# Nine of sixteen down stages computed with seven block products in place of eight

## The chip, the cores and the metric

One NeuronCore of a Trainium2 chip runs the kernel. The metric is device time in microseconds (us) of one execution; the time of a kernel is the median of its runs.

## The reference

The kernel computes one inference step of a decoder layer, for a prompt of 2048 tokens and 32 sample tokens, all in fp32 and 1024 wide. A mixing sub-layer comes first (one input projection, four mixers, one output projection). What matters here is the second half, a dense MLP with an inner width of 4096:

```python
f = rms_norm(x, g_ffn_pre)
f = jnp.square(jax.nn.relu(f @ w_up)) @ w_down      # (2048+32, 1024) @ (1024, 4096), then @ (4096, 1024)
x = x + rms_norm(f, g_ffn_post)
```

## The kernel before, in words

**Tiles and stages.** The prompt is cut into four blocks of 512 tokens (`b` = 0 to 3; the last block takes the 32 sample tokens with it). The inner width of 4096 is cut into four quarters of 1024 (`q` = 0 to 3). For each `b` and `q` there is a U stage, which makes u = relu(f @ w_up)² for 1024 inner columns, and a D stage, which multiplies u by the matching 1024 rows of w_down and adds the result to `f2_sb`. In the D stage of `q` = 3 the output projection of the next block is put in between. A U and a D stage together are called a round here.

**Panels.** Weights come in panels of 1024 rows by 256 columns (1 MB), four to a stage, in the order of the list `order`. A panel goes through the same steps in every stage: SyncE loads it to one of two buffers of `raw`; ScalarE (ACT) rounds it to `w_hi` (L702); VectorE (DVE) makes the rest, `w_lo` = `raw` - `w_hi` (L1161); TensorE (PE) takes both. `raw`, `w_hi` and `w_lo` each have two buffers, so the rounding of panel j+2 waits for the last matmul of panel j, and the load of panel j+2 for the subtraction of panel j.

**Products.** fp32 accuracy comes from three matmuls for each pair of tiles: high by high, low by high, high by low (`three`, L1873 to L1875). In the U stage the weights are stationary and 512 tokens move: a panel has 2 tiles of 128 inner columns, each 8 steps x 3 matmuls of 512 columns into one PSUM bank. ACT takes each bank through ReLU (L976) and square (L978) to one of two buffers `square`, DVE splits that into `u_hi` (a cast, L1564) and `u_lo` (L1568). In the D stage u is stationary and the 256 columns of w_down move: a panel is 4 token tiles x 8 steps x 3 = 96 matmuls, two token tiles to a bank, and a stage is 384 matmuls. DVE adds each bank to `f2_sb` (`d_add`, L1590); at `q` = 0 ACT copies instead (`d_copy`, L993).

**Order around the change.** Each engine runs a program written out by hand in its own order. In DVE's, `u_panel` and `token_panel` put the split of panel j+2 ahead of the last piece of panel j. Six PSUM banks (`mm`) are used in turn for U and D. GpSimd (POOL) computes nothing after the first microseconds; its queue only issues transfers: of the mixers' outputs (`mixc`, `mix_in`), of x and x2 to `x_in` (`rows_in`), of x2 and y to HBM (`results`). At the end of the first U stage come small steps for the 32 sample tokens, whose last result `conv_s` is stored from POOL's queue (L690); the first D stage waits for that store where `f2_sb` lies over the buffers of the first phase.

The functions that the diff touches, and their callers:

## Time and profile before

| | |
|---|---|
| median of 3 runs | 2186.59 us (2186.30 to 2190.09) |
| the profiled execution | 2184.32 us |
| its span, first to last instruction | 2182.4 us, granted clock 0.989 |
| PE busy / DVE busy / ACT busy / POOL busy | 96% / 50% / 35% / 5% |
| one U stage (`b` < 3), one D stage (`b` < 3, `q` < 3) | 44.15 us, 43.98 us |

A PE that is 96% busy leaves 87 us of the span in which no matmul runs. The lengths of the stages come from the timeline of PE, from the first matmul of a stage to the first of the next. Busy time counts overlapping matmuls once; the mean duration of one matmul is longer than the distance between two, since they are pipelined. DVE's and ACT's instructions don't overlap by more than 0.1 us, so their durations can be added.

### The profile page before, as it was taken

What the parts mean: (1) busy time and instruction counts of PE and PEld (TensorE: products, weight loads), DVE (VectorE), ACT (ScalarE), POOL (GpSimd) and SP (SyncE); (2) the same over time, 40 slices, a digit from 0 to 9 for tenths busy, and PEclk for the clock granted to TensorE, in tenths of its full rate; (3) what the DMA queues carried; (4) which work ended last, traced back from release to release, by engine and by line L of the source; (5) the groups of instructions that cost most, each with busy time, mean ns of one, the idle gap of its engine ahead of it and who ended that gap; (6) DMA issues with size and microseconds to landing.
All of it is one profiled execution on the core that took longest, in us unless ns stands there. A gap on an engine that the chain in (4) does not pass through costs nothing.

```text
span 2182.4 us, 32665 instructions
## 1 busy us (share of the span) xinstructions
PE 2095.6 (96%) x14201; PEld 1908.3 (87%) x14201; DVE 1099.4 (50%) x1505; ACT 754.7 (35%) x1160; POOL 107.7 (5%) x190
## 2 busy tenths in 40 slices
PE   6999999996999999999999999999999999999998
PEld 5877777786799898989898899899898989999998
DVE  3687777877623333564333346523334564334344
ACT  4424232234433323443323244332323443323142
POOL 2011111110000000000000000000000000000000
PEclk9999999997999999999999999999999999999999
DMA  7854656563232333344332344533333333222221
GB/s 254 284 212 161 223 178 213 174 204 126 70 118 96 97 97 126 131 149 155 97 97 97 97 136 155 170 101 97 97 97 118 108 108 136 94 81 84 92 78 61
DMA packets 184835, 287.40 MB, mean 132 GB/s; under 512 B 5967, under 2 KB 162292, under 8 KB 176484
## 3 DMA queue, kind: packets, MB, share of 16 engines
q1 hardware_dynamic: 160868, 169.99, 24.3%
q0 software_dynamic: 22784, 114.28, 14.9%
q8 instruction: 112, 1.84, 0.3%
q10 hardware_dynamic: 1040, 1.05, 0.1%
q14 instruction: 31, 0.25, 0.0%
HBM read 245.01 MB, written 40.57 MB: 131 GB/s over the span
## 4 chain that ended last, share of the span: by engine, by line
PE 65%; DVE 4%; ACT 3%; DMA 2%; issue 1%; POOL 0%; ACTq 0%; POOLq 0%; DVEq 0%
PE mm L1875 21%; PE mm L1873 21%; PE mm L1874 21%; DVE w_lo L1161 1%; ACT w_hi L702 1%; DMA mixc<-mixT_scratch 1%; PE mm L1882 1%; PE mm L1881 1%; DMA x_in<-in_x_prompt 0%; ACT junk_y L1003 0%; DVE conv_s L1779 0%; DVE f_sb L1590 0%; PE tr L2111 0%; ACT square L976 0%; DVE o_sb L1524 0%
## 5 line engine op out<-in xcount | busy, mean ns | idle before, releaser
L1161 DVE TENSOR_TENSOR w_lo<-raw,w_hi 128x2048 fp32r<-128x2048 f32 x152 | 348.5, 2293 | 644.6 <-ACT w_hi L702 644.6
L1873 PE MATMUL mm<-act_hi,w_hi 128*128 128x512 f32 (+2 forms) x1728 | 631.3, 365 | 8.1 <-DVE act_lo L1204 5.3
L1875 PE MATMUL mm<-act_hi,w_lo 128*128 128x512 f32 (+2 forms) x1728 | 631.0, 365 | 0.0
L1874 PE MATMUL mm<-act_lo,w_hi 128*128 128x512 f32 (+2 forms) x1728 | 624.7, 362 | 0.0
L1873 PE MATMUL mm<-w_hi,u_hi 128*128 128x256 f32 x2048 | 567.9, 277 | 1.7 <-DVE u_lo L1568 0.9
L1874 PE MATMUL mm<-w_lo,u_hi 128*128 128x256 f32 x2048 | 565.5, 276 | 0.0
L1875 PE MATMUL mm<-w_hi,u_lo 128*128 128x256 f32 x2048 | 565.4, 276 | 0.0
L702 ACT ACTIVATE w_hi<-raw 128x2048 fp32r<-128x2048 f32 x152 | 290.8, 1913 | 559.9 <-PE mm L1875 464.1
L1873 PEld LDWEIGHTS mm<-w_hi,u_hi 128*128 128x128 f32 x2048 | 384.4, 188 | 4.2 <-DVE u_lo L1568 3.8
L1874 PEld LDWEIGHTS mm<-w_lo,u_hi 128*128 128x128 f32 x2048 | 384.5, 188 | 0.5
L1875 PEld LDWEIGHTS mm<-w_hi,u_lo 128*128 128x128 f32 x2048 | 384.4, 188 | 0.0
L1873 PEld LDWEIGHTS mm<-act_hi,w_hi 128*128 128x128 f32 x1728 | 326.9, 189 | 60.2 <-issue 12.2
L1874 PEld LDWEIGHTS mm<-act_lo,w_hi 128*128 128x128 f32 x1728 | 327.0, 189 | 57.0 <-issue 2.4
L1875 PEld LDWEIGHTS mm<-act_hi,w_lo 128*128 128x128 f32 x1728 | 326.3, 189 | 50.7
L1873 PE MATMUL mm<-w_hi,act_hi 128*128 128x256 f32 x640 | 179.8, 281 | 7.5 <-DVE w_lo L1161 4.4
L1874 PE MATMUL mm<-w_lo,act_hi 128*128 128x256 f32 x640 | 178.0, 278 | 0.0
L1875 PE MATMUL mm<-w_hi,act_lo 128*128 128x256 f32 x640 | 178.0, 278 | 0.0
L976 ACT ACTIVATE square<-mm 128x512 f32<-128x512 f32 (+2 forms) x160 | 81.9, 512 | 244.5 <-PE mm L1875 237.6
L1215 DVE SCALAR_TENSOR_TENSOR conv<-g_ext,cst,conv 128x512 f32<-128x512 f32 x240 | 163.1, 746 | 0.7 <-ACT conv L826 0.7
L1564 DVE CAST u_hi<-square 128x512 fp32r<-128x512 f32 (+1 forms) x160 | 59.2, 370 | 145.1 <-ACT square L978 145.0
L1873 PEld LDWEIGHTS mm<-w_hi,act_hi 128*128 128x128 f32 x640 | 121.4, 190 | 8.9 <-DVE w_lo L1161 5.0
L1874 PEld LDWEIGHTS mm<-w_lo,act_hi 128*128 128x128 f32 x640 | 121.4, 190 | 0.6 <-issue 0.5
(269 smaller groups left out, 1512.8 us busy)
## 6 DMA issues: line engine op xcount, KB each, us to landing
raw<-in_w_ffn_up SPq DMA_DIRECT2D x64, 1024.0 KB, 5.3
raw<-in_w_ffn_down SPq DMA_DIRECT2D x64, 1024.0 KB, 5.2
w_hi<-whi_scratch POOLq DMA_DIRECT2D x24, 1024.0 KB, 5.2
w_lo<-wlo_scratch POOLq DMA_DIRECT2D x24, 1024.0 KB, 7.8
raw<-in_w_out SPq DMA_DIRECT2D x16, 1024.0 KB, 5.2
whi_scratch<-w_hi POOLq DMA_DIRECT2D x8, 1024.0 KB, 8.6
wlo_scratch<-w_lo POOLq DMA_DIRECT2D x8, 1024.0 KB, 10.7
mixc<-mixT_scratch POOLq DMA_DIRECT2D x16, 512.0 KB, 6.2
```

The costliest lines, as they stand in the source:

```text
L702: SC.activation(w_hi[:, s, :, :], raw[:, s, :, :], ACT.Copy).then_inc(hi_ready, 1)
L976: SC.activation(square[:, at % 2, 0:c1 - c0], mm[bank][:, 0:c1 - c0], ACT.Relu).then_inc(bank_free[bank], 1)
L1161: DVE.tensor_tensor(w_lo[:, s, :, :], raw[:, s, :, :], w_hi[:, s, :, :].bitcast(fp32), ALU.subtract)\
L1215: DVE.scalar_tensor_tensor(out=c, in0=g_ext[:, t, k:k + N1], scalar=col("conv_w", 2 * k + t), in1=c, op0=ALU.mult, op1=ALU.add).then_inc(c ...
L1564: DVE.tensor_copy(u_hi[:, k, c0:e], square[:, at % 2, 0:e - c0]).then_inc(u_hi_ready, 1)
L1873: PE.matmul(out, whi, xhi, start=(k == 0), stop=False)
L1874: PE.matmul(out, whi, xlo, start=False, stop=False)
L1875: return PE.matmul(out, wlo, xhi, start=False, stop=(k == K - 1))
L1881: PE.matmul(bank[0:2 * NS, 0:PC], x[:, k, :], whi, start=(k == 0), stop=False)
L1882: last = PE.matmul(bank[0:NS, 0:PC], x[:, k, 0:NS], wlo, start=False, stop=False)
```

## The change

In the D stages of `b` < 3 and `q` < 3 the product u @ w_down of 512 x 1024 by 1024 x 1024 is done by blocks. u is cut into 2 x 2 blocks A of 256 tokens by 512 inner rows (even tiles of 128 inner columns against odd ones), the weights into 2 x 2 blocks B of 512 inner rows by 512 columns. Winograd's form of Strassen's scheme then needs seven products of blocks, of these pairs:

| | left | right |
|---|---|---|
| part 0 | A11 | B11 |
| part 1 | S1 = A21 + A22 | T1 = B12 - B11 |
| part 2 | S2 = S1 - A11 | T2 = B22 - T1 |
| part 3 | A12 | B21 |
| part 4 | S3 = A11 - A21 | T3 = B22 - B12 |
| part 5 | S4 = A12 - S2 | B22 |
| part 6 | A22 | B21 - T2 (its sign is taken care of in the sums) |

Such a stage is called a W stage here. It has two halves (p = 0, 1) of 256 of each block's 512 columns, and seven products a half, each of 24 matmuls of 256 columns into one bank: 2 x 7 x 24 = 336 matmuls in place of 384. Who does what:

- SyncE loads eight pieces of 512 KB a stage in place of four of 1 MB.
- GpSimd makes the four sums of weight blocks of a half in place in `raw` (L764, L767, L769, L777), eight instructions of 128 x 1024 a stage.
- ACT and DVE split each part of the weights (128 x 1024) into high and low: 14 parts a stage, of which parts 0 and 1 of the first half lie at the end of the U stage's third panel.
- DVE makes the sums of u and splits all of them (`sums_1` to `sums_4`), in place of one cast and one subtraction a tile.
- DVE takes the products to seven sums `w_sum`, which lie in `f2_sb` and in `mixc`; at `q` = 0 it copies, ACT no longer does. `w_result` adds them up in the U stage of `q` = 3 (seven additions of 128 x 1024). The loads of `mixc` for the next block wait for that.
- The y tiles of the block before are done two each after panels 0 and 1 of the U stage, in place of one after each panel. The rest of the diff joins four semaphores to others and is left out below, as is the renumbering of buffers.

```diff
+        w_dn_7 = w_down[0].rearrange("(q k e p) c -> q e p k c", p=P, k=K // 2, e=2)
+        def wait_part(eng, j, i):
+            if i >= 4:
+                wait_bank(eng, j, i - 4)
+            elif order[j][3] == 1:
+                wait_bank(eng, j - 1, i + 3)
+            else:
+                wait_panel(eng, j - 2 + i // 2)
...
         @block.sync
+                        else:
+                            sp.wait_ge(lo_ready, split_no[j - 1] + 4)
+                            sp.dma_start(quarter(raw, b11), block_source(j, 0, 0)).then_inc(raw_full[b11], 16)
+                            sp.wait_ge(w_sums, 4 * w_no[j])
+                            sp.dma_start(quarter(raw, b12), block_source(j, 0, 1)).then_inc(raw_full[b12], 16)
+                            sp.wait_ge(lo_ready, split_no[j - 1] + 5)
+                            sp.dma_start(quarter(raw, b22), block_source(j, 1, 1)).then_inc(raw_full[b22], 16)
+                            sp.wait_ge(lo_ready, split_no[j - 1] + 6)
+                            sp.dma_start(quarter(raw, b21), block_source(j, 1, 0)).then_inc(raw_full[b21], 16)
...
+                    elif order[j - 1][0] == "W":
+                        sp.wait_ge(w_sums, 4 * (w_no[j - 1] + 1))
+                        sp.wait_ge(lo_ready, split_no[j - 1] + 5)
...
         @block.gpsimd
+            def weight_sums(j):
+                pool.wait_ge(raw_full[raw_at[j][2]], 16 * no12)
+                pool.wait_ge(lo_ready, split_no[j])
+                GP.tensor_tensor(b11, b12, b11, ALU.subtract).then_inc(w_sums, 1)
+                pool.wait_ge(raw_full[raw_at[j][3]], 16 * no22)
+                pool.wait_ge(w_sums, n + 1)
+                GP.tensor_tensor(b12, b22, b12, ALU.subtract).then_inc(w_sums, 1)
+                pool.wait_ge(lo_ready, split_no[j] + 1)
+                GP.tensor_tensor(b11, b22, b11, ALU.subtract).then_inc(w_sums, 1)
+            def weight_sum_4(j):
+                pool.wait_ge(w_sums, n + 3)
+                pool.wait_ge(lo_ready, split_no[j] + 3)
+                GP.tensor_tensor(b21, b21, b11, ALU.subtract).then_inc(w_sums, 1)
...
         @block.scalar
+            def part_hi(j, i):
+                wait_part(act, j, i)
...
+                if i in (1, 2, 4, 6):
+                    act.wait_ge(w_sums, 4 * w_no[j] + {1: 1, 2: 3, 4: 2, 6: 4}[i])
+                SC.activation(w_part(w_hi, j, i), raw_of_part(j, i), ACT.Copy).then_inc(hi_ready, 1)
...
             def u_panel(j):
+                if seven(b, q) and p >= NP - 2:
+                    squared_relu(j, 0)
+                    if p == NP - 2:
+                        part_hi(j + 2, 0)
+                    squared_relu(j, 1)
+                    if p == NP - 2:
+                        part_hi(j + 2, 1)
+                    return
...
         @block.vector
+            def sums_2(j):
+                dve.wait_ge(sq_ready, at + 2)
+                DVE.tensor_tensor(s1, even[:, 2 * P:4 * P], odd[:, 2 * P:4 * P], ALU.add).then_inc(u_hi_ready, 1)
...
+                DVE.tensor_tensor(s2, s1, even[:, 0:2 * P], ALU.subtract).then_inc(u_hi_ready, 1)
...
+                block_parts(s1, s_hi[:, 0, p, :], s_lo[:, 0, p, :])
+                DVE.tensor_tensor(s4, odd[:, 0:2 * P], s2, ALU.subtract).then_inc(u_hi_ready, 1)
...
+                block_parts(s2, s_hi[:, 1, p, :], s_lo[:, 1, p, :])
...
+            def w_add(j, i):
+                wait_bank(dve, j, i)
+                if q == 0:
+                    if b > 0:
+                        dve.wait_ge(y_out, 16 * NCH * b)
+                    else:
...
+                        dve.wait_ge(smp_st, 64)
+                    DVE.tensor_copy(dst, src).then_inc(bank_free[bank], 1)
+                else:
...
+                    DVE.tensor_tensor(dst, src, dst, ALU.add).then_inc(bank_free[bank], 1)
...
         @block.tensor
+            def w_products(j):
+                for i, (hi, lo, far) in enumerate(w_u):
+                    bank = take_bank(j, i)
+                    pe.wait_ge(lo_ready, split_no[j] + i)
+                    if p == 0:
+                        pe.wait_ge(u_lo_ready, u_before[j - 1] + far)
+                    whi, wlo = w_part(w_hi, j, i), w_part(w_lo, j, i)
+                    for h in range(2):
+                        for k in range(K // 2):
+                            PE.matmul(out, hi[:, k, t], whi[:, k, :], start=(k == 0), stop=False)
+                            PE.matmul(out, lo[:, k, t], whi[:, k, :], start=False, stop=False)
+                            last = PE.matmul(out, hi[:, k, t], wlo[:, k, :], start=False, stop=(k == K // 2 - 1))
+                    last.then_inc(bank_done[bank], 1)
```

On DVE, half of a D stage of `q` > 0 of the kernel before is this (L1161 splits a panel, L1590 adds a bank):

```order
L1590 TENSOR_TENSOR f_sb<-mm,f_sb 128x2x256 [waits bank_done2,bank_free4]
L1161 TENSOR_TENSOR w_lo<-raw,w_hi 128x2048 [waits hi_ready]
L1590 TENSOR_TENSOR f_sb<-mm,f_sb 128x2x256 [waits bank_done3,bank_free5]
L1590 TENSOR_TENSOR f_sb<-mm,f_sb 128x2x256 [waits bank_done4,bank_free0]
L1161 TENSOR_TENSOR w_lo<-raw,w_hi 128x2048 [waits hi_ready]
L1590 TENSOR_TENSOR f_sb<-mm,f_sb 128x2x256 [waits bank_done5,bank_free1]
```

which are two panels of the four. On the same engine of the changed kernel, from the first row that waits for the last tile of the U stage to the split of part 4, whose end lets the load of the second half's first block go (L1797 to L1802 with L1771 and L1773 are `sums_2`, L1358 is `part_lo`, L1839 is `w_add`, the a_hi and s_hi rows after it are `sums_3` and `sums_4`):

```order
L1797 TENSOR_TENSOR s_sum<-square 128x256 [waits sq_ready]
L1799 TENSOR_TENSOR s_sum<-s_sum,square 128x256 [waits u_hi_ready]
...
L1358 TENSOR_TENSOR w_lo<-raw,w_hi 128x1024 [waits hi_ready]
L1839 TENSOR_TENSOR f_sb<-mm,f_sb 128x2x256 [waits bank_free4,bank_done2]
L1771 CAST a_hi<-square 128x256
L1773 TENSOR_TENSOR a_lo<-square,a_hi 128x256 [waits u_hi_ready]
L1358 TENSOR_TENSOR w_lo<-raw,w_hi 128x1024 [waits hi_ready]
L1839 TENSOR_TENSOR f_sb<-mm,f_sb 128x2x256 [waits bank_free5,bank_done3]
L1771 CAST s_hi<-s_sum 128x2x256
L1773 TENSOR_TENSOR s_lo<-s_sum,s_hi 128x2x256 [waits u_hi_ready]
L1771 CAST a_hi<-square 128x256
L1773 TENSOR_TENSOR a_lo<-square,a_hi 128x256 [waits u_hi_ready]
L1358 TENSOR_TENSOR w_lo<-raw,w_hi 128x1024 [waits hi_ready]
```

Where a panel had one split and two additions for 96 matmuls, there is now one split and one addition for each 24, and the last sums of u lie between the first of them. On POOL, the first half of the first W stage; the kernel before has only the two DMA rows here:

```order
L781 DMA mixT_scratch<-us_sb 128x2x32 [waits smp_y2]
L764 TENSOR_TENSOR raw<-raw 128x1024 [waits lo_ready,raw_full2]
L767 TENSOR_TENSOR raw<-raw 128x1024 [waits w_sums,raw_full3]
L769 TENSOR_TENSOR raw<-raw 128x1024 [waits lo_ready]
L781 DMA mixT_scratch<-conv_s 128x2x32 [waits smp_y1]
L777 TENSOR_TENSOR raw<-raw 128x1024 [waits lo_ready,w_sums]
```

The first, third and fourth sum wait for a split on DVE, and the splits of parts 1, 2, 4 and 6 on ACT wait for sums. The store of `conv_s` now has three sums ahead of it.

## Rows read from the trace of the kernel before

**Rows 1.** Busy time of each engine over the span (the page's part 1).

```profile
PE 2095.6 (96%) x14201; PEld 1908.3 (87%) x14201; DVE 1099.4 (50%) x1505; ACT 754.7 (35%) x1160; POOL 107.7 (5%) x190
```

**Rows 2.** The chain that ended last, by engine (the page's part 4).

```profile
PE 65%; DVE 4%; ACT 3%; DMA 2%; issue 1%; POOL 0%; ACTq 0%; POOLq 0%; DVEq 0%
```

**Rows 3.** Windows U, U, D: length; busy PE, PEld, DVE, ACT, POOL; clock.

```profile
954.79:998.94 44.15, 44.15 (x194) 36.07 (x193) 24.68 (x27) 17.04 (x23) 2.66 (x5) 1.00 0.47 155
1042.89:1087.05 44.16, 44.16 (x194) 36.08 (x193) 16.74 (x18) 16.43 (x19) 0.00 (x0) 1.00 0.30 96
1087.05:1131.03 43.98, 43.83 (x386) 43.63 (x384) 14.86 (x13) 8.79 (x6) 0.00 (x0) 1.00 0.31 96
```

**Rows 4.** Timeline where U ends and D begins: start, length, what.

```profile
1086.82 0.39 PE L1875 MATMUL mm<-act_hi,w_lo 128*128 128x512 f32 x1
...
1087.05 0.28 PE L1873 MATMUL mm<-w_hi,u_hi 128*128 128x256 f32 x1
...
1087.25 0.60 ACT L976 ACTIVATE square<-mm 128x512 f32<-128x512 f32 x1 [4.25 <-PE mm L1875]
...
1087.40 0.28 PE L1873 MATMUL mm<-w_hi,u_hi 128*128 128x256 f32 x1
```

**Rows 5.** Groups by line and shape: count, busy us, mean ns, idle before.

```profile
L1161 DVE TENSOR_TENSOR w_lo<-raw,w_hi 128x2048 fp32r<-128x2048 f32 x152 | 348.5, 2293 | 644.6 <-ACT w_hi L702 644.6
...
L702 ACT ACTIVATE w_hi<-raw 128x2048 fp32r<-128x2048 f32 x152 | 290.8, 1913 | 559.9 <-PE mm L1875 464.1 <-PE mm L1884 88.6 <-DMA wlo_scratch<-w_lo 6.4
...
L1590 DVE TENSOR_TENSOR f_sb<-mm,f_sb 128x512 f32<-128x512 f32 x96 | 66.0, 688 | 71.6 <-PE mm L1875 71.5
L978 ACT ACTIVATE square<-square 128x512 f32<-128x512 f32 x96 | 60.8, 633 | 3.0
L976 ACT ACTIVATE square<-mm 128x512 f32<-128x512 f32 x96 | 56.7, 590 | 165.7 <-PE mm L1875 161.5 <-issue 4.3
L1564 DVE CAST u_hi<-square 128x512 fp32r<-128x512 f32 x96 | 40.7, 424 | 120.2 <-ACT square L978 120.2
...
L1568 DVE TENSOR_TENSOR u_lo<-square,u_hi 128x256 fp32r<-128x256 f32 x64 | 27.0, 422 | 1.1
...
L1489 DVE TENSOR_TENSOR act_lo<-mixc,act_hi 128x1024 fp32r<-128x1024 f32 x16 | 19.2, 1223 | 24.6 <-ACT act_hi L927 24.6
...
L1564 DVE CAST u_hi<-square 128x256 fp32r<-128x256 f32 x64 | 18.4, 288 | 24.9 <-ACT square L978 24.8
...
L927 ACT ACTIVATE act_hi<-mixc 128x1024 fp32r<-128x1024 f32 x16 | 16.5, 1053 | 33.6 <-DMA mixc<-mixT_scratch 33.6
```

**Rows 6.** GpSimd's memsets and selects by shape, same columns.

```profile
L584 POOL TENSOR_SCALAR_AFFINE_SELECT v_n<-v_n 128x512 f32<-128x512 f32 x1 | 1.0, 968 | 1.9 <-DMA v_n<-in_sgu_w 1.9
...
L564 POOL MEMSET wpool<- 128x256 f32 x1 | 0.3, 331 | 0.0
...
L568 POOL TENSOR_SCALAR_AFFINE_SELECT ident<-ident 128x128 f32<-128x128 f32 x1 | 0.3, 289 | 0.2 <-POOL sgu_wS L566 0.2
L562 POOL MEMSET ident<- 128x128 f32 x1 | 0.2, 224 | 0.0
```

**Rows 7.** Timeline of DVE and GpSimd at 11 us.

```profile
11.10 1.28 DVE L1197 SCALAR_TENSOR_TENSOR x<-x,x_stats,gpre 128x1024 f32<-128x1024 f32 x1
...
11.92 0.97 POOL L584 TENSOR_SCALAR_AFFINE_SELECT v_n<-v_n 128x512 f32<-128x512 f32 x1 [1.87 <-DMA v_n<-in_sgu_w]
```

**Rows 8.** Transfers: queue, count, KB each, median us from issue to landing.

```profile
raw<-in_w_ffn_up SPq DMA_DIRECT2D x64, 1024.0 KB, 5.3
...
x_scratch<-o_sb POOLq DMA_DIRECT2D x12, 512.0 KB, 3.2
...
out<-f_sb SPq DMA_DIRECT2D x4, 512.0 KB, 2.7
...
mixT_scratch<-us_sb POOLq DMA_DIRECT2D x1, 32.0 KB, 2.0
```

**Rows 9.** POOL's timeline in the first D stage (from 594.03).

```profile
603.08 0.73 POOL L690 DMA_DIRECT2D mixT_scratch<-conv_s  x1 [36.03 <-DVE conv_s L1823]
```

More of the change, by code:

```diff
@@ L49, in hybrid_trunk_step @@
             order += [("U", b, q, p) for p in range(NP)]
-            if q < Q - 1 or b == NB - 1:
+            if seven(b, q):
+                order += [("W", b, q, p) for p in range(NP // 2)]
+            elif b == NB - 1:
                 order += [("D", b, q, p) for p in range(NP)]
@@ L83, in hybrid_trunk_step @@
         kind, b, q, p = order[j]
+        if kind == "W":
+            for i in range(NS7):
+                bank = (turn - 2 * NP + 4) % NRING
+                turn += 1
+                wrote[bank] += 1
+                bank_of[j, i] = (bank, wrote[bank], freed[bank])
+                freed[bank] += 1
+            bank_of[j, "last"] = bank_of[j, NS7 - 1]
+            continue
         n_banks = 2 * len(halves(b)) if kind == "U" else len(token_banks(b))
@@ L1133, in _ @@
                                 sample_swish()
-                    if q < Q - 1:
+                    if seven(b, q):
+                        for p in range(NP // 2):
+                            w_panel(index("W", b, q, p))
+                    elif q < Q - 1:
                         for p in range(NP):
@@ new lines, in sums_3, with sums_4 @@
+            def sums_3(j):
+                p = order[j][3]
+                block_parts(square[:, 1, 0:2 * P], a12_hi[:, p, :], a12_lo[:, p, :])
+            def sums_4(j):
+                p = order[j][3]
+                block_parts(s_sum[:, 2:4, :], s_hi[:, 2:4, p, :], s_lo[:, 2:4, p, :])
+                block_parts(square[:, 1, 2 * P:4 * P], a22_hi[:, p, :], a22_lo[:, p, :])
+            extra = [f2_sb[:, NCH, :]] + [mixc[:, i, :, :].rearrange("p k t -> p (k t)") for i in range(2)]
+            m1, m6, m7 = (x.rearrange("p (h c) -> p h c", h=2) for x in extra)
@@ L1576, in d_add @@
                 f2 = f2_sb[0:n, tile:tile + nt, p * PC:(p + 1) * PC]
-                if q > 0:
+                if q > 0 and not seven(b, q - 1):
                     old, _, free = bank_of[index("D", b, q - 1, p), i]
@@ L1639, in u_panel @@
                 n = 2 * len(halves(b))
+                if seven(b, q):
+                    sums_1(j)
+                    if p < NP - 2:
+                        split_lo(j + 2)
+                    if p == NP - 2:
+                        part_lo(j + 2, 0)
+                    sums_2(j)
+                    if p < NP - 1:
+                        sums_3(j)
+                        sums_4(j)
+                    if p == NP - 2:
+                        part_lo(j + 2, 1)
+                    return
                 for i in range(n):
@@ L1846, in _ @@
                             sample_taps(range(22, TAPS))
[L1847 removed]
+                    if seven(b, q):
+                        for p in range(NP // 2):
+                            w_panel(index("W", b, q, p))
+                    elif q < Q - 1:
                         for p in range(NP):
```

291 lines of the change are left out of this document (245 added, 46 removed).

## The prediction

> **What bounds the kernel now.** I read the page's busy times first: PE is busy for 2095.6 of 2182.4 us, DVE for half of the span, GpSimd for 5% [rows 1]. The chain of waits agrees: 65% of it is PE, and no other engine has over 4% [rows 2]. The windows by stage then show where it matters here. A U stage takes 44.16 us and PE is busy throughout; a D stage takes 43.98 us with 0.15 us idle, at full clock; DVE has 16.7 and 14.9 us of work in them, GpSimd none [rows 3]. So a round of U and D lasts 88.14 us, PE sets all of it, and matmuls left out would be time saved, as long as the work that replaces them is ready when PE wants it.
>
> **What the change takes away.** A D stage is 384 matmuls in 43.98 us, 0.1145 us each; the timeline shows three in 0.35 us at its start [rows 3, 4]. The seven products are 336 matmuls of the same form (u stationary, 256 columns), 38.5 us. That is 5.5 us less in each of nine stages, 49.5 us in all, if nothing is late. A product, 24 matmuls, lasts 2.75 us.
>
> **What it adds, by engine.** ACT: 14 casts of 128 x 1024 a stage at 1.05 us and two panels of the next U stage at 1.91, 18.6 us in 38.5; there is room [rows 5]. Its copies at q = 0 go to DVE. DVE, for each panel of U: subtractions and additions of 256 columns at 0.42 and casts at 0.29 make 0.71 for a split of 256 columns, and 0.42 + 0.69 = 1.11 for one of 512 [rows 5]. `sums_1` is 0.42 + 0.71 = 1.1, `sums_2` three sums and two splits, 2.7, `sums_3` 0.7, `sums_4` 1.1 + 0.7 = 1.8; together 6.3, four times a round. The parts are 14 x 1.22, the additions of products 14 x 0.69, the U panels 4 x 2.29. A round is 25.4 + 17.1 + 9.7 + 9.2 = 61 us of DVE, where it was 31.6, in the 82.7 us that PE would need. GpSimd: eight sums a round. The trace of before has no two-input instruction there. Its memsets of 256 and 128 columns differ by 0.107 us, 0.84 ns a column, over a fixed 0.12 [rows 6]. A sum has two reads and a write. Counted as two such passes it takes 0.12 + 1.72 = 1.85 us, as three 2.7. I take the middle, 2.3, since reads and the write may or may not overlap, and keep both ends. Eight of them are 18 us a round; GpSimd's own time is no bound.
>
> **Do DVE and GpSimd work side by side?** The trace has one place that bears on it. At 11.92 us GpSimd began a select of 128 x 512, one input, while DVE was in a two-input instruction until 12.38 [rows 7]. It took 0.968 us. The select of 128 columns, alone, took 0.289; at the memset's slope 512 columns would take 0.289 + 0.32 = 0.61 [rows 6]. It was 0.36 longer, against 0.46 of overlap. That looks like GpSimd waiting for DVE's instruction to end. It can also be read as a slope of 1.77 ns a column for the select, and DVE, which was first, lost nothing (1.28 us). I take the first reading: two such instructions take turns, whichever started first. The Trainium skill (SBUF — State Buffer, Who interferes with whom) says the same of a VectorE instruction with two SBUF inputs against a GpSimd one that reads SBUF; by it alone the turn also holds the other way, with DVE waiting, which no row here shows. The skill (GPSIMD Engine Reference, Elementwise — side-by-side cycle accounting) has 4497 ns for a two-input sum of 2048 columns; an estimate from that page is 2.2 us for 1024, and the loss below would be about 1 us a stage smaller.
>
> **One round, step by step.** Zero is the end of the U stage. Handoffs are 0.2 to 0.3 us from PE (ACT began 0.2 after the D stage did, [rows 4]) and under 0.1 between the others.
> 1. ACT casts part 0 when panel 2 of U is done (-11.0), then does ReLU and square of its last tile (0.59 + 0.63, [rows 5]), so DVE can start `sums_2` of that panel at -8.4. To the u block that the first product needs it then has 2.7 + 0.7 + 1.8, part 1 (1.2) and `sums_1` of panel 3 (1.1): 7.5 us, done at -0.9. With no turns PE doesn't wait. But GpSimd's first three sums fall here (after part 0, after the first, after part 1). With turns they add 6.9 us: the first product starts at **+6.0**.
> 2. From there DVE has `sums_2` of panel 3 (2.7), parts 2 and 3 (2.4), two additions (1.4), `sums_3` (0.7), GpSimd's fourth sum (2.3), `sums_4` (1.8), part 4 (1.2): 12.5, less 0.3 where instructions join without a gap. Product 4 is due after four products, at 11.0; it waits 1.2.
> 3. Only the end of part 4 lets SyncE load the second half's first block. 512 KB landed in 2.7 and 3.2 us, 1 MB in 5.3 [rows 8]; I take 3.3. Then comes a chain in which nothing overlaps: load 3.4, cast 1.05, subtraction 1.2, sum 1 2.3, sum 2 2.3 (it is next on GpSimd's queue, and DVE's part 1, whose cast ran beside it, waits its turn), part 1 1.2, sum 3 2.3, cast 1.05, part 2 1.2, handoffs 0.4: 16.4. Part 2 is ready 28.6 after the first product; with nine products done it was due at 24.8 + 1.2. PE waits 2.6.
> 4. From there: part 3 (1.2), sum 4 (2.3), parts 4 and 5 with an addition between (3.1), which frees the buffer for the next U panel; load 5.4, cast 1.9, subtraction 2.3: 16.2. The next U stage starts 44.8 after the first product, at 50.8. PE's queue holds all later stages behind that wait.
>
> The W stage then lasts 50.8 us where D took 43.98: **6.8 us more, 61 in nine stages**. With 1.85 us for a sum the same walk loses three times 0.45 in step 1 and five times in steps 2 to 4, about 3.6: 3.2 more a stage, 29 in all. With 2.7 us it is 10 more, 90 in all.
>
> **Once only.** In the first W stage DVE's first addition waits for the store of `conv_s`. That was issued at 603.08, 9.05 after the stage began [rows 9], and a like store landed in 2.0 us [rows 8]; so 11.1, where the addition would else be at 5.6: 5.5 late, with all splits behind it; 6 us. At q = 0 of b = 1 and 2 the y tiles are done in two panels in place of four. DVE had 24.68 - 16.74 = 7.9 us more there [rows 3]. Panels 0 and 1 are then 28 us of DVE from 7.0 on, and it is 6 us late at panel 2, where 4.4 are idle: 1.6 each, 3 in all. `w_result`, seven times 1.22, lies in a U stage of q = 3 with 17 us of DVE work in 44: nothing; without that cover it would be 8.5 a block. The loads of `mixc` that wait for it have three panels, 33 us, ahead of their use.
>
> **Sum.** 2184.3 (the profiled execution) + 61 + 6 + 3 = 2254; the median of the runs stands 2.3 above that execution, so 2257. A measurement of this kernel can tell 0.2%, 4.4 us, from no change.
>
> **The rivals.**
> - *They do work side by side.* For it: DVE's instruction lost nothing [rows 7]. Step 1 costs nothing but 0.6 us at the second product, whose S1 is ready 3.3 us after the last tile. Step 2 ends at 11.4; the chain of step 3 has the cast of part 1 (1.05) where sum 2 stood (2.3), 15.2 us, and gives part 2 at 26.6; with the addition of product 2 behind that (to 30.3), part 5 (1.2) and step 4's 9.6 the U stage starts at 41.2. That is 2.8 us less a stage: -25 + 9 = -16, **2171**. It decides where the three sums of step 1 hold DVE for under about 2 us in all. This is the case on the other side.
> - *Only casts wait.* A cast of 512 columns takes 0.424 us where a two-input instruction takes 0.69 [rows 5], so it moves two columns at a time and may need a path that the others don't. Then each sum delays DVE to its next cast only: the first product at +4.0, the next U stage at 45.4: 1.4 more a stage, 13 + 9 = 22, **2208**.
> - *Everything is hidden.* If sums take 1 us, loads 2.7 and nothing waits, step 4's load is still about 1 us late for the U stage, but up to 4 us a stage stay: 36 to 49 us, **2145**.
> That the products aren't seven is excluded by the order on PE.
>
> **Chances.** Turns 0.47, casts only 0.14, side by side 0.29, all hidden 0.10. Faster: the last two, less 0.02 where the once-only terms eat the gain: 0.37. Same: 0.05, from the edges of the second and third. Slower: 0.58. Both signs hold much, so the range spans them: 2150 leaves out most of the last case, 2282 the long end of the first (with 2.7 us a sum it is 2286). The likeliest case's own range is 2225 to 2286.
>
> **What would show it.** Right: GpSimd's sums at 2 to 2.7 us alone and longer beside DVE; DVE subtractions of 256 columns that read 2 us and more; PE idle for about 6 us where a W stage begins, until a DVE a_lo; W stages of 50 to 51 us; idle PE before the next U stage until w_lo, L1353. Wrong in the mechanism: subtractions still at 0.42 and 1.22 us beside a running sum, and a first product on time. Wrong in size: DVE idle for microseconds in the W stage while it waits for ACT, behind loads over 4 us.

## The result, and the profile after

| | before | changed |
|---|---|---|
| median of four runs each | 2186.55 us | 2283.01 us (2280.23 to 2289.67) |
| ratio | | 1.0442, 95% interval 1.0416 to 1.0467 |
| profiled execution, and its span | 2184.32, 2182.4 | 2289.67, 2287.9 |

The change makes the kernel slower by 4.4%, 96.5 us. The forecast was 2257 us with a range to 2282; the sign and the mechanism are as forecast, the loss is 1.4 times as large. The page of the changed kernel, first its busy times, then the slices (granted clock) and the loads:

```profile
PE 2097.6 (92%) x13769; PEld 1902.7 (83%) x13769; DVE 1464.7 (64%) x2126; ACT 803.4 (35%) x1226; POOL 281.1 (12%) x262
...
PEclk9999999997899999998999999999999999999999
...
PE 43%; DVE 19%; DMA 5%; ACT 5%; issue 2%; POOL 2%; ACTq 0%; DVEq 0%; POOLq 0%; SPq 0%
...
raw<-in_w_ffn_up SPq DMA_DIRECT2D x64, 1024.0 KB, 5.3
raw<-in_w_ffn_down SPq DMA_DIRECT2D x72, 512.0 KB, 5.0
```

PE is as busy as before [rows 1], though it has 432 matmuls fewer: these were worth 49.5 us, and PE's work did not fall. That is the first surprise. In the chain, DVE has gone from 4% [rows 2] to 19%. What PE waits for, by releaser (total, times, longest):

```profile
PE mm L2511 <- DVE a_lo L1773: 53.9, 9, 11.2
PE mm L2511 <- DVE w_lo L1358: 30.1, 20, 3.1
PE mm L2214 <- DVE w_lo L1353: 16.7, 12, 2.6
...
PE tr L2229 <- DVE conv_s L2114: 9.2, 1, 9.2
```

The first three are the waits that the prediction names: ahead of the first product, inside the second half, ahead of the next U stage. The fourth it does not have. Of the signs that the prediction gave, those for its mechanism are all there, and so is one for a wrong size: in the W stage below DVE waits 1.9 us for ACT, behind a load of 4.2 us. The windows of block 1, q = 1 (U stage; PE's wait; the first product alone; the whole W stage from its first product; the columns are those of [rows 3]; a wait ahead of a first product is counted here from the start of the U stage's last matmul):

```profile
1094.81:1138.90 44.09, 44.09 (x192) 35.99 (x192) 30.15 (x52) 15.05 (x19) 4.89 (x2) 1.00 0.30 96
1138.90:1144.28 5.38, 0.35 (x2) 0.03 (x1) 5.28 (x8) 1.89 (x3) 2.45 (x1) 0.80 0.00 0
1144.28:1149.20 4.92, 4.92 (x24) 4.92 (x25) 3.52 (x8) 1.34 (x2) 0.00 (x0) 0.52 0.00 0
1144.28:1191.23 46.95, 43.20 (x336) 42.66 (x336) 33.19 (x39) 14.01 (x14) 11.97 (x5) 0.91 0.28 90
```

The W stage's 336 matmuls take 43.2 us, not the 38.5 that the matmuls of a D stage would give [rows 3, 4]. The third row says why: after the wait the granted clock is 0.52 on the mean, nearly all the time at the lower of the two levels (1.2 GHz), and a product takes 4.92 us in place of 2.75. The next one takes 2.72. The Trainium skill (TensorE: Matmul & The Clock Gate, Part 1: The HAM clock gate) says that an idle TensorE falls back to 1.2 GHz, and this trace agrees; the forecast had no term for it.

What DVE and GpSimd do beside each other, from the timeline of the same stage (start, length, engine, line):

```profile
1130.49 0.42 DVE L1797 TENSOR_TENSOR s_sum<-square 128x256 f32<-128x256 f32 x1
1130.71 2.47 POOL L764 TENSOR_TENSOR raw<-raw 128x1024 f32<-128x1024 f32 x1 [48.38 <-DVE w_lo L1358]
1130.95 2.51 DVE L1799 TENSOR_TENSOR s_sum<-s_sum,square 128x256 f32<-128x256 f32 x1
1133.32 2.42 POOL L767 TENSOR_TENSOR raw<-raw 128x1024 f32<-128x1024 f32 x1
1133.49 2.39 DVE L1771 CAST s_hi<-s_sum 128x256 fp32r<-128x256 f32 x1
...
1164.10 2.40 POOL L764 TENSOR_TENSOR raw<-raw 128x1024 f32<-128x1024 f32 x1 [9.57 <-DVE w_lo L1358]
1164.47 0.68 DVE L1839 TENSOR_TENSOR f_sb<-mm,f_sb 128x512 f32<-128x512 f32 x1
```

A subtraction of 0.42 us takes 2.51, a cast of 0.29 us takes 2.39, and each ends within 0.3 us of GpSimd's sum. The last two rows are the exception: an addition with one operand in PSUM, 0.68 us beside a running sum. A split of 1.22 us that starts beside a sum takes as long as what is left of the sum and then 1.08 us more:

```profile
1167.68 2.44 DVE L1358 TENSOR_TENSOR w_lo<-raw,w_hi 128x1024 fp32r<-128x1024 f32 x1 [2.53 <-ACT w_hi L873]
```

In all, the eight sums of this stage hold VectorE off for 10.9 us, not for eight times 2.4, since some find it idle or adding from PSUM. Ahead of the first product VectorE has no idle time at all from 1130.5 on, so the 6.2 us by which three of its instructions are stretched there cover the whole of PE's wait. GpSimd's own sums are hardly stretched:

```profile
L764 POOL TENSOR_TENSOR raw<-raw 128x1024 f32<-128x1024 f32 x18 | 43.7, 2430 | 406.3 <-DVE w_lo L1358 406.3
L767 POOL TENSOR_TENSOR raw<-raw 128x1024 f32<-128x1024 f32 x18 | 43.1, 2395 | 2.6
```

By stretches, from the profiled executions (the time of PE's first matmul of each stage). "Forecast" is what the prediction's steps give for the same stretch.

| stretch | before | after | more | forecast |
|---|---|---|---|---|
| six rounds of q = 1 and 2 | 528.8 | 583.1 | 54.3 | 41 |
| two rounds of q = 0, blocks 1 and 2 | 176.2 | 206.7 | 30.5 | 17 |
| start to the end of the first W stage | 637.7 | 656.6 | 18.9 | 13 |
| all the rest | 839.7 | 841.5 | 1.8 | 0 |
| span | 2182.4 | 2287.9 | 105.5 | 70 |

### The profile page after: what moved, and what is told of

It is laid out like the page before. It is cut to its first block, busy times and chain, and to the rows that moved or that the text cites. A ratio compares the mean times of both kernels' runs of the same rounds, so it can differ in the third digit from the quotient of the medians.

```text
span 2287.9 us, 32917 instructions
## 1 busy us (share of the span) xinstructions
PE 2097.6 (92%) x13769; PEld 1902.7 (83%) x13769; DVE 1464.7 (64%) x2126; ACT 803.4 (35%) x1226; POOL 281.1 (12%) x262
## 4 chain that ended last, share of the span: by engine, by line
PE 43%; DVE 19%; DMA 5%; ACT 5%; issue 2%; POOL 2%; ACTq 0%; DVEq 0%; POOLq 0%; SPq 0%
PE mm L2214 13%; PE mm L2216 12%; PE mm L2215 12%; DVE w_lo L1358 4%; DVE w_lo L1353 3%; DVE s_hi L1771 2%; DMA raw<-in_w_ffn_up 2%; ACT w_hi L859 2%; DMA raw<-in_w_ffn_down 2%; ACT w_hi L873 2%; DVE s_lo L1773 1%; PE mm L2511 1%; DVE a_hi L1771 1%; PE mm L2512 1%; DVE s_sum L1799 1%
## 5 line engine op out<-in xcount | busy, mean ns | idle before, releaser
L2214 PE MATMUL mm<-act_hi,w_hi 128*128 128x512 f32 (+2 forms) x1728 | 635.0, 367 | 19.2 <-DVE w_lo L1353 12.3
L2214 PE MATMUL mm<-w_hi,u_hi 128*128 128x256 f32 x896 | 248.8, 278 | 0.4
L2215 PE MATMUL mm<-w_lo,u_hi 128*128 128x256 f32 x896 | 247.4, 276 | 0.0
L2216 PE MATMUL mm<-w_hi,u_lo 128*128 128x256 f32 x896 | 247.4, 276 | 0.0
L873 ACT ACTIVATE w_hi<-raw 128x1024 fp32r<-128x1024 f32 x126 | 129.3, 1055 | 309.7 <-POOL raw L764 80.9
L1358 DVE TENSOR_TENSOR w_lo<-raw,w_hi 128x1024 fp32r<-128x1024 f32 x126 | 180.5, 1438 | 74.8 <-ACT w_hi L873 74.8
L2511 PE MATMUL mm<-w_hi,s_hi 128*128 128x256 f32 x576 | 167.8, 291 | 32.1 <-DVE w_lo L1358 29.7
L2511 PE MATMUL mm<-w_hi,a_hi 128*128 128x256 f32 x432 | 128.7, 298 | 54.3 <-DVE a_lo L1773 53.9
L2214 PEld LDWEIGHTS mm<-w_hi,u_hi 128*128 128x128 f32 x896 | 168.2, 188 | 1.1 <-DVE u_lo L1766 1.0
L2215 PEld LDWEIGHTS mm<-w_lo,u_hi 128*128 128x128 f32 x896 | 168.2, 188 | 0.1
L2216 PEld LDWEIGHTS mm<-w_hi,u_lo 128*128 128x128 f32 x896 | 168.2, 188 | 0.0
```

Source lines behind the costliest of these rows:

```text
L873: SC.activation(w_part(w_hi, j, i), raw_of_part(j, i), ACT.Copy).then_inc(hi_ready, 1)
L1358: DVE.tensor_tensor(w_part(w_lo, j, i), raw_of_part(j, i), w_part(w_hi, j, i).bitcast(fp32), ALU.subtract).then_inc(lo_ready, 1)
L2214: PE.matmul(out, whi, xhi, start=(k == 0), stop=False)
L2215: PE.matmul(out, whi, xlo, start=False, stop=False)
L2216: return PE.matmul(out, wlo, xhi, start=False, stop=(k == K - 1))
L2511: PE.matmul(out, hi[:, k, t], whi[:, k, :], start=(k == 0), stop=False)
```

## The experiments

Each run's time is a median beside runs of the kernel before on the same chip, 2186.0 to 2187.2 us in the four batches.

**1. The sums on VectorE.** GpSimd's four sums of a half become VectorE instructions at the places where they would have been done.

```diff
-                GP.tensor_tensor(b11, b12, b11, ALU.subtract).then_inc(w_sums, 1)
...
+                DVE.tensor_tensor(out, x, y, ALU.subtract).then_inc(w_sums, 1)
...
                         part_lo(j + 2, 0)
+                        block_sum(j + 2, 1)
+                        block_sum(j + 2, 2)
```

> All eight weight sums of a W stage are VectorE instructions, at the same places of the order where GpSimd would have finished them; everything else is the change. Theory (a running GpSimd sum holds VectorE off for its 2.4 us): the sums take 1.22 us of VectorE in place of 2.4 us of holding it off, so the first product starts about 2.8 us after the U stage instead of 5.4, the second half's part 2 is ready 27.4 after it, the next U stage starts 43 after it. W stages of 45 to 46 us counted from the U stage's end, where they are 52.3 now; 2205 to 2220 us. Rival (nothing is held off, VectorE simply has too much work and PE waits for that): 9.8 us more VectorE work a round make it longer still, 2290 to 2330 us.

Measured: 2235.81 us, ratio 1.0216 (1.0200 to 1.0232), 47 us less than the change. The round of block 1, q = 1:

```profile
1073.46:1117.50 44.04, 44.04 (x192) 35.98 (x192) 29.95 (x57) 15.48 (x19) 0.00 (x0) 1.00 0.30 96
1117.50:1120.69 3.19, 0.39 (x2) 0.03 (x1) 3.02 (x6) 2.40 (x4) 0.00 (x0) 0.98 0.00 0
1120.69:1163.75 43.06, 40.48 (x337) 39.94 (x337) 34.33 (x44) 13.04 (x12) 0.00 (x0) 0.96 0.31 99
```

The wait is 3.2 us (2.8 expected) and the W stage counted from the U stage's end 46.25 us (45 to 46 expected); the rival, in which VectorE's 9.8 us more work a round add to the time, is out. VectorE is busy for 67.3 us of this round and was for 68.6 in the change: eight sums of 1.22 us take nearly what the holds took. What is gained lies where everything waits for one sum after another, ahead of the first product and at the start of the second half. The total is 16 us above the range expected. By stretches of the profiled executions, the six rounds of q = 1 and 2 give back 37.6 us, the two of q = 0 12.1 (they still have a wait of 9.4 us) and the part up to the end of the first W stage only 3.9.

**2. Sums of 8 elements.** The same GpSimd instructions and waits, with the weight sums left out but for 8 elements a partition.

```diff
-                GP.tensor_tensor(b11, b12, b11, ALU.subtract).then_inc(w_sums, 1)
+                GP.tensor_tensor(b11[:, 0, 0:8], b12[:, 0, 0:8], b11[:, 0, 0:8], ALU.subtract).then_inc(w_sums, 1)
```

> The four GpSimd sums of a half stay in place with their waits, but each touches 8 elements a partition in place of 1024, so the weight sums are left out but for these elements. Theory (the sums' 2.4 us on GpSimd, in the chain and in front of VectorE, are the loss): first product within 1 us of the U stage's end, no wait for part 2 in the second half, W stages of 38.5 to 40 us, 2150 to 2165 us. Rival (the 512 KB loads of 5.0 us are what makes the second half late): a wait of 2 us and more stays in the second half and before the next U stage, W stages of 43 us and more, 2190 us or more.

Measured: 2183.56 us, 0.9984 (0.9973 to 0.9995), and this round:

```profile
1047.71:1091.97 44.26, 44.26 (x192) 36.18 (x193) 29.17 (x58) 15.48 (x19) 0.90 (x3) 1.00 0.30 95
1091.97:1131.75 39.78, 38.51 (x338) 38.15 (x336) 28.60 (x39) 16.09 (x16) 1.02 (x5) 1.00 0.33 107
```

The first product starts on time, the clock stays at 1.00, the matmuls take their 38.51 us, and the second half has no wait although the loads still land in 5.0 us. VectorE is busy for 57.8 us of the round, 10.8 less than in the change. So of a W stage's loss all is the sums, directly or through the clock; how much is VectorE held off and how much the sum's own length in the chain of the second half, this run doesn't part. But the total missed: 2150 to 2165 was expected. The six rounds of q = 1 and 2 are 22.9 us shorter than before; the two of q = 0 are 7.3 us longer, the stretch to the end of the first W stage 11.05. These 18 us don't come from the sums (run 5, with none on GpSimd, has 5.9 and 11.3 there); the forecast's once-only terms (9 us) were thought to lie on top of the waits of a W stage, and are there without any.

**3. PE kept busy.** Transposes of the identity into an unused bank, with no wait of their own, ahead of three products.

```diff
+            def idle_work(n):
+                for _ in range(n):
+                    PE.transpose(tr[0][:, 0:P], ident[:, :], ident[:, :])
...
+                    idle_work({(0, 0): 44, (1, 1): 30, (1, 2): 18}.get((p, i), 0))
                     bank = take_bank(j, i)
```

> Transposes of the constant identity into an unused bank are put in PE's order ahead of three waits of a W stage (44 ahead of the first product, 30 and 18 ahead of the second half's second and third), nothing else changes. The trace of the change shows PE's matmuls at 0.213 us in place of 0.107 for some 4 us after each long pause, 43.1 us of PE work in a W stage in place of 38.5. Theory (the granted clock falls in the pauses, the slow products cost only where VectorE waits for product 0 and 1 after them, about 1.9 us a stage): clock 0.99, W products at full speed, longer waits in their place, 2262 to 2272 us. Rival (the slow clock is worth its full 4.6 us a stage): 2240 us. Rival (the clock has nothing to do with the pauses): 2283 us or more, slow products still there.

Measured: 2272.19 us, 1.0390 (1.0374 to 1.0405), 10.8 us less than the change. The first matmuls after the wait, and the window of a W stage, wait included:

```profile
1140.89 0.36 PE L2516 MATMUL mm<-w_hi,a_hi 128*128 128x256 f32 x1 [0.26 <-DVE a_lo L1773]
1141.09 0.28 PE L2517 MATMUL mm<-w_hi,a_lo 128*128 128x256 f32 x1
1141.20 0.28 PE L2518 MATMUL mm<-w_lo,a_hi 128*128 128x256 f32 x1
...
1135.67:1186.45 50.78, 49.33 (x429) 48.75 (x427) 38.47 (x46) 16.24 (x16) 14.44 (x6) 1.00 0.26 84
```

The matmuls now follow each other by 0.11 us at once, and the clock is 1.00. So it was the pauses that lowered it. Of the 4.7 us of slow matmuls a stage only 1.2 come back (this round is 95.1 us where it was 96.4). Most slow matmuls lie in time that PE would have waited. What costs is the slow first product: VectorE's first addition waits for it, and with VectorE the load of the second half. The same addition in the change and here:

```profile
1149.49 0.69 DVE L1839 TENSOR_TENSOR f_sb<-mm,f_sb 128x512 f32<-128x512 f32 x1 [1.52 <-PE mm L2513]
...
1144.50 0.69 DVE L1839 TENSOR_TENSOR f_sb<-mm,f_sb 128x512 f32<-128x512 f32 x1
```

The split of part 4, which lets that load go, ends 13.1 us after the first product in the change and 11.5 here. The 1.2 us are a lower bound: the transposes in the second half last longer than the waits that they fill. The second half's second product starts at 1167.02, 2.5 us after its split was done, the third at 1171.81, 2.5 after its own, and VectorE then waits 0.74 us for PE.

**4. A copy and a memset on GpSimd** in place of the weight sums, which are left out; they tell what kind of instruction holds VectorE off.

```diff
-                GP.tensor_tensor(b11, b12, b11, ALU.subtract).then_inc(w_sums, 1)
+                GP.tensor_copy(b11, b12).then_inc(w_sums, 1)
...
-                GP.tensor_tensor(b12, b22, b12, ALU.subtract).then_inc(w_sums, 1)
+                GP.memset(b12, 0.0).then_inc(w_sums, 1)
```

> In place of the weight sums GpSimd does, at the same places and with the same waits, a copy of 128 x 1024 (first and third), which reads one operand, and a memset of 128 x 1024 (second and fourth), which reads none; the weight sums are left out. Theory (what holds VectorE off is GpSimd's instruction with two SBUF operands): VectorE's casts and subtractions beside the memset take their 0.29 to 1.22 us unstretched, those beside the copy perhaps. Rival (any GpSimd instruction on SBUF holds off VectorE's instructions whose operands all lie in SBUF): casts and subtractions stretch beside the memset too, by what is left of its 1.0 us.

Measured: one execution, 2185.29 us. Two places of its timeline:

```profile
1122.45 0.96 POOL L777 MEMSET raw<- 128x1024 f32 x1 [3.67 <-DVE w_lo L1358]
1122.85 1.21 DVE L1358 TENSOR_TENSOR w_lo<-raw,w_hi 128x1024 fp32r<-128x1024 f32 x1
...
1171.82 1.12 POOL L764 COPY raw<-raw 128x1024 f32<-128x1024 f32 x1 [48.41 <-DVE w_lo L1358]
1172.07 1.14 DVE L1799 TENSOR_TENSOR s_sum<-s_sum,square 128x256 f32<-128x256 f32 x1
1173.06 0.95 POOL L767 MEMSET raw<- 128x1024 f32 x1
1173.25 0.91 DVE L1771 CAST s_hi<-s_sum 128x256 fp32r<-128x256 f32 x1
```

Neither expectation holds as put. A copy, with one operand, holds off a two-input VectorE instruction (0.42 us becomes 1.14). A memset holds off a cast (0.29 becomes 0.91), but a two-input subtraction beside it takes its plain 1.21. The Trainium skill (SBUF — State Buffer, Who interferes with whom) has just this: two SBUF inputs clash with a GpSimd instruction that reads, not with one that only writes; a cast can enter a two-port mode, which clashes with any; an instruction with at most one input in SBUF, outside that mode, clashes with none. This trace agrees on all four (beside a copy, an addition from PSUM takes 0.68 us). The page adds that whoever comes first has the ports. Here it was always GpSimd that had them; where a sum began 0.2 us before a VectorE instruction's end it took 2.47 us in place of 2.39, too little to tell.

**5. VectorE's order.** The run with the sums on VectorE, its queue rewritten: in the U stage part 1 and sum 3 behind the last panel's first split, sum 2 later; in the W stage parts ahead of additions.

```diff
                 if order[j][3] == 0:
                     part_lo(j, 2)
-                    w_add(j, 0)
                     sums_3(j - 1)
                     part_lo(j, 3)
-                    block_sum(j, 4)
-                    w_add(j, 1)
+                    block_sum(j, 2)
                     sums_4(j - 1)
                     part_lo(j, 4)
-                    w_add(j, 2)
                     part_lo(j, 5)
-                    w_add(j, 3)
+                    block_sum(j, 4)
+                    w_add(j, 0)
+                    w_add(j, 1)
                     part_lo(j, 6)
+                    w_add(j, 2)
...
+                    if p == NP - 1:
+                        part_lo(j + 1, 1)
+                        block_sum(j + 1, 3)
                     sums_2(j)
```

> The run with the weight sums on VectorE, with VectorE's order rewritten by when PE needs each thing: part 1 and sum 3 behind the last panel's first split, sum 2 later, parts 2 to 5 ahead of the additions, the second half's parts ahead of what its products wait for. Theory (with nothing held off, what is left of the loss, 3.2 us ahead of the first product and 1 to 2 us in the second half, is VectorE's order): the first product within 0.5 us of the U stage's end, W stages of 40 to 43 us, rounds of 85 to 87 us where that run has 90.3; 2200 to 2210 us. Rival (VectorE has too much to do in a round whatever the order): rounds of 89 us and more, 2230 us or more.

Measured: 2184.59 us, 0.9992 (0.9982 to 1.0001): no difference from before, 51 us less than the first order and 15 less than the lower end of what was expected.

```profile
1051.71:1095.98 44.27, 44.27 (x193) 36.20 (x193) 30.80 (x60) 16.14 (x19) 0.00 (x0) 1.00 0.29 95
1095.98:1136.64 40.66, 39.93 (x338) 39.56 (x336) 36.24 (x46) 15.56 (x16) 0.00 (x0) 1.00 0.33 105
```

A round is 84.9 us where the kernel before has 88.1 [rows 3]. VectorE is busy for 36 of 41 us in the W stage and still on time. The rounds of q = 0 are 91.4 and 90.7 us: with the y tiles VectorE is late, and the first product waits for it for 5.6 us.

**6. The order alone.** The change with GpSimd's sums, and that order (GpSimd's second and third sum exchanged).

```diff
                     if p == NP - 2:
                         part_lo(j + 2, 0)
+                    if p == NP - 1:
+                        part_lo(j + 1, 1)
                     sums_2(j)
```

> The change, GpSimd's sums and all, with VectorE's order rewritten as in the run with sums on VectorE, and GpSimd's second and third sum exchanged. It tells the engine from the order. Theory (each sum holds VectorE off for up to 2.4 us, where one on VectorE costs it 1.22, so the order can't make it good): rounds of 90 to 94 us, between the change's 96.3 and the 84.8 of the reordered run with sums on VectorE; 2230 to 2265 us. Rival (the order alone was at fault, the engine makes no difference): rounds of 86 us or less, 2195 us or less.

Measured: 2265.10 us, 1.0362 (1.0346 to 1.0378), a round of 94.05 us:

```profile
1084.34:1128.62 44.28, 44.28 (x193) 36.07 (x193) 30.87 (x59) 15.87 (x19) 2.47 (x1) 1.00 0.30 95
1128.62:1178.39 49.77, 40.92 (x337) 40.18 (x336) 37.93 (x39) 16.25 (x16) 17.64 (x7) 0.97 0.26 85
```

The first product now starts on time, but the second waits 4.3 us, for an s_lo ahead of which two sums of u were held off, 2.27 and 2.46 us in place of 0.42 each; in the second half PE waits 3.0 us. Engine and order are worth 47 and 18 us each without the other and 98 together: while sums on GpSimd hold VectorE off, a better order moves the wait to the next product.

**7. y tiles one per panel**, with the sums on VectorE, reordered.

```diff
-                        if b > 0 and q == 0 and p < 2:
+                        if b > 0 and q == 0:
                             if p == 0:
                                 y_inverse(b - 1)
-                            y_tile(b - 1, 2 * p)
-                            y_tile(b - 1, 2 * p + 1)
+                            y_tile(b - 1, p)
```

> As the run before, and the four y tiles of q = 0 stand one behind each U panel, as in the kernel before, in place of two behind each of the first two. Theory (in the change two y tiles at a time push VectorE behind, while its idle time further on is lost, 11.6 us ahead of the first product where it is 5.4 elsewhere): the U stages of q = 0 end with 4 to 8 us less wait in each of two rounds, 8 to 16 us less in all. Rival (10 us of y tiles a round cost the same wherever they stand): no difference.

Measured: 2184.21 us, 0.9989 (0.9979 to 0.9998): no difference, the rival. In block 1 the wait ahead of the first product falls from 5.6 to 3.2 us, and the W stage has waits of 1.4 and 0.7 us in its place. It is the work that doesn't fit, not its place.

**8. No W stage in the first block**, GpSimd's sums as in the change.

```diff
-        return b < NB - 1 and q < Q - 1
+        return 0 < b < NB - 1 and q < Q - 1
```

> The change in the second and third block alone: six W stages with GpSimd's sums, the first block's three are D stages again. The trace of the change has its first three rounds 18.9, 9.8 and 7.8 us longer than before. Theory (a third or so of the loss lies in the first block, 12 us of it ahead of the first product, where VectorE also has the sample's work): 2283 less 37, 2243 to 2250 us. Rival (each W stage costs the same 7 to 8 us and the first block only 6 more, as forecast): 2253 to 2258 us.

Measured: 2248.48 us, 1.0282 (1.0267 to 1.0297), 34.5 us less than the change, as expected: the three W stages of the first block cost 34.5, where the forecast's steps had 26.

**9. Six W stages, sums on VectorE, reordered**, in blocks 1 and 2 alone (the edits of 7 and 8 together).

> The run with y tiles one per panel, with W stages in the second and third block alone. Theory (a round of 85 to 87 us in place of 88.1 and no first round with the sample's work in it): six rounds with 1 to 3 us less each, 2170 to 2182 us, faster than before. Rival (at q = 0 the y tiles still make those two rounds longer than before by 3 us or more): within 4 us of 2186.

Measured: 2183.21 us, 0.9983 (0.9974 to 0.9992), within 4 us of before: the rival. The two rounds of q = 0 take 91.6 us against 88.1, 7.0 us more, and eat most of the 10.3 that the four others gain.

**10. W stages at q = 1 and 2 alone.** At q = 0 the down stage stays as before. Its four quarters lie where products 4, 6, 7 and 2 of the seven are summed, so these are added to them; the second product goes into two quarters of the result, hence one subtraction at the start.

```diff
+                if q == 1 and i in (0, 2, 4):
                     DVE.tensor_copy(dst, src).then_inc(bank_free[bank], 1)
                 else:
...
+            def w_start(b):
...
+                DVE.tensor_tensor(m3, m3, m5, ALU.subtract).then_inc(u_hi_ready, 1)
```

> Sums on VectorE, its order rewritten, y tiles one per panel; W stages at q = 1 and 2 of the three blocks alone, six of them. At q = 0 the down stage is the one of the kernel before, its partial results are what four of the seven products are then added to, after one subtraction of 128 x 1024. Theory (a W stage is worth 3.3 us a round where VectorE has no other work, and nothing or less where it has the y tiles or the sample): six times 3.3 less, 2166 to 2171 us, faster than before by 0.7 to 0.9%. Rival (the wait of the first addition for the sample's store, or w_start and w_result, take it back): 2178 us or more.

Measured: **2169.55 us, 0.9928 (0.9915 to 0.9940)**, faster than both kernels. Block 1's q = 0 round, then its first round with a W stage (U and W apart):

```profile
949.43:1037.56 88.13, 87.98 (x578) 79.70 (x577) 37.39 (x35) 29.54 (x36) 3.19 (x6) 1.00 0.40 132
1037.56:1081.71 44.15, 44.15 (x194) 36.07 (x193) 30.33 (x58) 16.62 (x20) 0.00 (x0) 1.00 0.23 72
1081.71:1123.51 41.80, 39.72 (x338) 38.80 (x336) 36.29 (x46) 15.76 (x16) 0.00 (x0) 1.00 0.31 101
```

**11 and 12. The first block's load alone**, in the change and in run 10.

```diff
                             sp.dma_start(quarter(raw, b11), block_source(j, 0, 0)).then_inc(raw_full[b11], 16)
+                            sp.wait_ge(raw_full[b11], 16 * raw_no[j][0])
```

> The change with one wait more on SyncE: in the second half of a W stage the loads of the other three blocks are issued only when the first block's 512 KB has landed, where they follow it by 0.4 to 3.5 us in the change and the 72 loads of 512 KB land in 5.0 us (median). Theory (the load is slow because others share the DMA queues with it): alone it lands in 3.2 to 3.5 us, the half's part 0 is ready 1 us earlier, but the second block lands up to 2 us later and its sum with it: 2275 to 2290 us. Rival (a load of 512 KB from these rows takes 4 us and more by itself): it lands in over 4 us, and the time is 2290 us or more.

> The same wait in the run with W stages at q = 1 and 2. There the second half's third product waits 1.0 us, behind part 2, which needs the first block's load, cast and split and then sum 1, which also needs the second block's load. Theory (the first block's landing sets that wait): 0.5 us less a stage, 2166 us. Rival (the second block's landing, now later, sets it): 1 to 2 us more a stage, 2175 to 2182 us.

Measured: 2302.19 us, 1.0533 (1.0510 to 1.0556), and 2176.10 us, 0.9958 (0.9944 to 0.9972). Issue to the next issue, which waits for nothing but the landing, in the first:

```profile
1160.38 0.37 SPq L618 DMA_DIRECT2D raw<-in_w_ffn_down  x1
1164.35 0.37 SPq L621 DMA_DIRECT2D raw<-in_w_ffn_down  x1
```

Alone the 512 KB land in 3.97 us, not in the 3.2 to 3.5 that the theory had. The theory was also wrong about the load that it would speed up. 5.0 us is the median of all 72 loads; the first block's (L618) are, but for one, not among the slow ones. Their landing in the change and in run 11, least, median and most:

```profile
DMA to landing us min/median/max: 4.0/4.2/6.7
...
DMA to landing us min/median/max: 4.0/4.0/4.1
```

So there were 0.2 us to gain, and the second block's later landing costs 19 and 6.5 us: the rivals, both times. The Trainium skill (DMA: Bandwidth & Descriptors, Anatomy of one DMA — SWDGE (gpsimd) path) fits 2.0 us plus the bytes at 436 GB/s, 3.2 us for 512 KB by an estimate; that is for another path than SyncE's, and the 3.97 us decide here.

## Why the prediction was right in sign and too small

**Right.** *What the change takes away*: 38.51 us for 336 matmuls at full clock (run 2). *Turns*: VectorE is held off by 6.2 us in step 1 (2.51, 2.39 and 2.31 us where 0.42, 0.29 and 0.29 stand otherwise); the forecast had 6.9 and a first product at +6.0, it came at +5.4. The sum alone takes 2.40 us where 2.3 was taken. The side-by-side rival is out by the rows, and so is the one in which a sum delays only casts: sums and subtractions with both operands in SBUF wait too. What the rule lacked is that additions from PSUM don't wait. `w_result` cost nothing: the U stages of q = 3 are 44.3 us.

**Step 2 and the clock: a term that was missing.** The prediction counted every matmul at 0.1145 us, from stages in which PE never pauses, although it forecast pauses, and so put the clock at nothing. The first product behind the wait takes 4.9 us in place of 2.75, VectorE's first addition waits 1.52 us for it, and part 4 is ready at 13.1 where step 2 had 12.2; at full clock (run 3) it is ready at 11.5. The wait of 1.2 us at product 4 is not there, as product 0 is late itself; in run 3 it is 0.4. In the round above PE waits 5.38 + 3.75 = 9.1 us where the steps had 12.3, but its matmuls take 4.7 us more; together 1.5 us more a round. Run 3 gives 1.2 us a stage, as a lower bound, for the clock.

**Step 3: a load and three sums mis-sized.** 3.3 us was taken from rows of stores of 512 KB [rows 8]; the second half's first block lands in 4.2 (median of nine). It is the kernel's long serial chain, so these 0.9 us stand in it in full, and so do three sums of 2.40 for 2.3: from part 4, whose end lets the load go, to part 2 it is 17.7 us where the steps had 16.4. Part of that is hidden by the slow products ahead: PE is idle for 1.3 and 1.9 us in the second half of that stage where 2.6 was forecast. Step 4 was right: 16.2 us from there to the next U stage.

**Once only: wrong in size, and it holds without the sums.** These terms miss about 15 of the 35 us of the profiled executions that are summed up below. At q = 0 the prediction packed VectorE's work without gaps: panels 0 and 1 "28 us of DVE from 7.0 on", so ready at 35. VectorE's order is fixed, and between a panel's first split and the next split of weights it stands still for 4.7 us, waiting for ACT's cast. It is done at 39.5 in run 2, and the lateness is 5.2 us (run 2) to 6.2 (a wait of 11.6 against 5.4 in the change), not 1.6. The first round had its 6 us for the store of `conv_s`. That store is worth about half of it: the addition that waits for it comes 8.5 us after the first product, not 11.1. What the term missed is that the sample's taps, 8.2 us of small instructions, now stand behind more of VectorE's work, while PE's transposes wait for them: 9.2 us at L2229, where the kernel before waits 2.6.

The six rounds of q = 1 and 2 lose 9.05 us on the mean: three 7.8 to 8.3, two 9.7 and 9.8, one 11.0. Their excess over the 6.8 forecast is 13.5 us in all; q = 0 adds 13.6, the first round 6, the rest 2: the 35 us by which 105.5 exceeds 70. The two rounds at 9.7 and 9.8 follow W stages of q = 0. PE waits 2.3 and 2.6 us ahead of their U stages, and these run at 0.96 of the clock and last 1.5 us longer:

```profile
656.60:702.20 45.60, 45.60 (x191) 37.16 (x192) 30.15 (x52) 15.42 (x19) 4.88 (x2) 0.96 0.29 93
1531.43:1577.00 45.57, 45.57 (x192) 37.13 (x192) 30.12 (x52) 14.55 (x19) 4.89 (x2) 0.96 0.28 92
```

In the round at 11.0 the second half's first block lands in 6.7 us, the one slow landing of nine, and PE waits 3.1 us for part 1; why that load was slow stays open. The profiled execution was the slowest of the four, up to 9 us longer than the others, so by the medians the forecast misses 26 us and not 35.

The chances stand as they were drawn: the likeliest case happened, at the far end of its own range (2225 to 2286). The whole range ended at 2282 because its upper end was made of one unknown alone, a sum of 2.7 us; it held no bound for VectorE's idle time at q = 0, for the sample's taps, for matmuls at the lower clock, or for a longer load. That 2283 lies so near to 2282 is no merit of the terms: some were too large (the turn of sum 4 with its full length, the store), others too small or missing.

## What to carry to other kernels

A GpSimd instruction on SBUF isn't free for VectorE: the next VectorE instruction with two SBUF inputs, or the next cast in SBUF, waits until it ends. Price it so, and compare that with the same work on VectorE (up to 2.4 against 1.22 us here). A saving on the bounding engine is worth what the feeding engine can deliver in order, so write the feeding engine's queue by due times and use the trick only where that engine has room (q = 1 and 2 here: 0.7% faster). When a forecast puts waits on TensorE, add the slow matmuls behind each, but only as far as another engine waits for their result. Size a load by rows of that very shape and place, not by the median of a mixed group, and pack an engine's work only as densely as its fixed order allows.

## What the runs showed of the hardware that was not expected

- The granted clock can fall to its lower level behind waits of a few microseconds: it is 0.52 in the product after 5.4 us of waiting. It need not: behind a wait of 3.2 us in run 1 it is 0.50 over the first 3 us at q = 1 of block 1 and 1.00 over the same stretch at q = 2. After waits of 0.4 and 0.8 us in run 2 it stays at 1.00.
- A GpSimd memset holds off a VectorE cast, but not a two-input subtraction (run 4). A GpSimd two-input sum of 8 elements takes 0.19 to 0.32 us (run 2), one of 1024 elements 2.40, a copy of 1024 elements 1.04 to 1.17 and a memset of them 0.96 (run 4).
- A load of 512 KB in rows of 1 KB needs 4.0 us alone (run 11), hardly less than the 5.1 to 5.3 us of 1 MB. The first of four issued close together lands in 4.2 us, the third in 5.4 (the change).
